# Two expert blocks kept on chip and added by one-hot products, the other rows summed earlier

## What is computed

```python
def hier_moe(x, w_r1, b_r1, w_r2, b_r2, w_gate, w_up, w_down):
    # top-1 group, then top-2 experts of that group: two (expert, gate) pairs for every token
    ...
    def run_block(args):                      # a block: rows of one expert
        tok, e = args
        xb = xpad[tok]
        hidden = jax.nn.silu(xb @ w_gate[e]) * (xb @ w_up[e])
        return hidden @ w_down[e]
    yb = lax.map(run_block, (row_tok.reshape(n_blocks, MOE_BLOCK), blk_expert))
    y = segment_sum(yb * row_gate[:, None], row_tok)[:T]     # each token: sum of its two rows

# for each layer i:
#   x = x + mixer_i(rms_norm(x));  x = x + hier_moe(rms_norm(x))
```

## Time and profile before

| | |
|---|---|
| runs | 1470.32, 1470.36, 1471.22 us (median 1470.36) |
| the profiled execution | 1471.15 us; span of its instructions 1469.2 us |
| busy | PE 88%, DVE 23%, ACT 21%, POOL 16% |
| memory | 464 MB read, 28 MB written, 335 GB/s over the span |
| TensorE's granted clock, mean | 0.946 of full |

### The profile page before, as it was taken

One profiled execution on the slowest core, in us unless ns is written; L12 is line 12 of the kernel. 1 busy time (PEld: TensorE's weight loads), 2 busy tenths in 40 slices (PEclk: granted clock), 3 DMA queues, 4 the chain that ended last, 5 costly groups with the idle time before them and its releaser, 6 DMA issues. The chain is left out here.

```text
span 1469.2 us, 17145 instructions
## 1 busy us (share of the span) xinstructions
PE 1286.6 (88%) x6316; PEld 650.9 (44%) x6316; DVE 344.4 (23%) x719; ACT 308.6 (21%) x638; POOL 233.3 (16%) x391
## 2 busy tenths in 40 slices
PE   9999888888878889999998999999978887888782
PEld 7643333333333333678776544643333343333331
DVE  4621100000000003654317543611000000000003
ACT  4211111111111113343335432211111111111110
POOL 1111111111111102033232220111111111111100
PEclk9999999999999999999999999999998999999997
DMA  9799999999999998412047213999999999999995
GB/s 370 280 361 396 401 397 407 414 412 402 409 408 407 399 415 321 145 58 88 31 136 258 77 31 138 386 375 398 399 406 408 409 411 413 412 404 401 405 401 206
DMA packets 57484, 477.39 MB, mean 325 GB/s; under 512 B 11373, under 2 KB 12653, under 8 KB 31258
## 3 DMA queue, kind: packets, MB, share of 16 engines
q1 hardware_dynamic: 39134, 433.74, 73.5%
q0 software_dynamic: 15504, 33.98, 7.3%
q10 hardware_dynamic: 2796, 8.97, 1.7%
HBM read 464.34 MB, written 28.04 MB: 335 GB/s over the span
## 5 line engine op out<-in xcount | busy, mean ns | idle before, releaser
L1774 PE MATMUL ps<-ring,xT 128*64 128x512 f32 x352 | 182.2, 678 | 48.9 <-issue 40.5
L1444 DVE SCALAR_TENSOR_TENSOR nat<-nat,slot_gate,ps 64x512 f32<-64x512 f32 x64 | 47.3, 739 | 664.9 <-ACT nat L1004 664.7
L1774 PE MATMUL ps<-pair,xT 128*64 128x512 f32 x352 | 169.9, 640 | 37.2 <-DMA pair<-in_moe_w_up 37.2
L1774 PE MATMUL ps<-third_pair,xT 128*64 128x512 f32 x320 | 156.9, 648 | 45.5 <-issue 25.1
L1775 PE MATMUL ps<-ring,xT 128*64 128x512 f32 x352 | 182.6, 679 | 0.0
L707 POOL DMA_INDIRECT yb<-nat,scol x64 | 59.4, 928 | 775.0 <-DVE nat L1440 775.0
L1775 PE MATMUL ps<-pair,xT 128*64 128x512 f32 x352 | 170.4, 641 | 0.0
L1004 ACT ACTIVATE nat<-ps 64x512 f32<-64x512 f32 x64 | 38.0, 594 | 609.5 <-PE ps L1775 609.5
L1775 PE MATMUL ps<-third_pair,xT 128*64 128x512 f32 x320 | 157.3, 649 | 0.0
L1783 PE MATMUL ps<-qk,hidT 128*64 128x512 f32 x336 | 153.1, 598 | 1.2 <-ACT hidT L981 1.2
L1784 PE MATMUL ps<-qk,hidT 128*64 128x512 f32 x336 | 153.2, 598 | 0.0
(11 more groups left out here) (226 smaller groups left out, 1833.0 us busy)
## 6 DMA issues: line engine op xcount, KB each, us to landing
qk<-in_moe_w_down SPq DMA_DIRECT2D x42, 2048.0 KB, 40.1
ring<-in_moe_w_down SPq DMA_DIRECT2D x22, 2048.0 KB, 40.1
pair<-in_moe_w_gate SPq DMA_DIRECT2D x22, 2048.0 KB, 34.6
pair<-in_moe_w_up SPq DMA_DIRECT2D x22, 2048.0 KB, 39.1
ring<-in_moe_w_gate SPq DMA_DIRECT2D x20, 2048.0 KB, 34.4
ring<-in_moe_w_up SPq DMA_DIRECT2D x20, 2048.0 KB, 38.9
third_pair<-in_moe_w_gate SPq DMA_DIRECT2D x20, 2048.0 KB, 34.9
third_pair<-in_moe_w_up SPq DMA_DIRECT2D x20, 2048.0 KB, 39.4
```

The lines of the kernel that those rows point to most:

```text
L1444: return V.scalar_tensor_tensor(out=hidden, in0=silu, scalar=slot_gate[:, bass.ds(j, 1)], in1=ps[0:BLK, GU_BANK, :], op0=ALU.mult, op1=ALU ...
L1774: mm(ps[BLK:P, GU_BANK, :], rows, gate[:, at], start=(k == 0), stop=(k == KT - 1))
```

## The change

1. The last two blocks of each layer, 30 and 31, are no longer scattered. Block 30's rows go to partitions 0 to 63 of `late_y` (a part of `nat`), block 31's to partitions 64 to 127. For each token tile, PE multiplies a one-hot matrix of 128 slots by the tile's tokens (`late_hot`) with `late_y`, two products of 128x512, and DVE adds the result from PSUM to `x` (`late_sum`). DVE builds the one-hot matrix in block 1 (`late_rows`, seven small operations).
2. Since rows of those two experts are no longer written to `yb`, the buffer has to hold zeros there: `yb` is cleared by two DMAs for a layer (`cleared`, 1088 rows, 4.46 MB). Layer 0's stand on SP's queue behind the inputs and before the first weights; layer 1's stand before the fourth piece of `w_qkv`. They read zeros that POOL writes by a memset.
3. POOL raises `rows_scattered` when block 29's rows have landed. `load_rows` loads tiles 0, 1 and 3 then, and tiles 2 and 4 once block 30's result is there. There are five buffers now. In layer 0 the loads stand before the second piece of `w_qkv`, and not before the third; the third waits for `x_done` of three tiles.
4. The sum of a token's two rows is made by DVE for tiles 0, 2 and 4 (`early_sum`) and by POOL for tiles 1 and 3 (`POOL_TILES`); DVE adds it to `x`. In layer 0 these sums stand between the quarters of `split_att`.
5. In layer 0, 12 of 18 `keep_busy` products go, three tiles' one-hot products come in their place, and the other two tiles' stand inside the first product.

```diff
-        yc = [nat[:, 0:2 * D], nat[:, 2 * D:4 * D], qk_flat[:, route_at:route_at + 2 * D], rows_h[:, 3:5, :].rearrange(
-            "p a d -> p (a d)")]
-        assert NT == len(yc) + 1
+        yc = [third_pair[:, 0, 0:2 * D], third_pair[:, 0, 2 * D:4 * D], ring[:, 2, 0:2 * D],
+              qk_flat[:, 2 * KT * T - SLOT:2 * KT * T - 2 * D], qk_flat[:, 2 * KT * T - 2 * D:2 * KT * T]]
+        assert NT == len(yc) and 2 * KT * T - SLOT >= NT * D - D and SLOT == 4 * D
+        LATE = 2
+        late_y = nat[:, 2 * D:3 * D]
+        assert LATE * BLK == P and (NEXP - LATE) % 2 == 0
...
+        zeros = early_rows[:, 3 * D:4 * D]
+        late_hot = ffn_gain[:, 0:NT * P]
+        late_iota = ffn_gain[:, NT * P:(NT + 1) * P]
+        late_at = ffn_gain[:, (NT + 1) * P:(NT + 1) * P + NT]
...
+        POOL_TILES = (1, 3)
+
+        def cleared(l, zero):
+
+            whole = YROWS // P * P
+            return [(yb_dram[l][0:whole, :].rearrange("(p k) d -> p k d", p=P),
+                     zero.unsqueeze(1).broadcast_to((P, YROWS // P, D))),
+                    (yb_dram[l][whole:YROWS, :], zero[0:YROWS - whole, :])]
+
+        def late_bank(l, i):
+
+            return 2 * (i % 4) if l == 1 else 2 * min(i, 2)
+
+        def late_bank_free(l, i):
+
+            return (i - 3 if i > 3 else 0) if l == 1 else (i if i > 2 else 0)
...
+            sp.wait_ge(zeroed, 1)
+            for rows, source in cleared(0, zeros):
+                sp.dma_start(rows, source).then_inc(yb_cleared, 16)
...
                 sp.wait_ge(rows_scattered, l + 1)
-                for i in range(NT):
+                for i in (0, 1, 3, 2, 4):
                     n = ROWS[i]
-                    if i >= len(yc):
-
-                        sp.wait_ge(x_done[l], i - len(yc) + 1)
-                    sp.dma_start(yc[i % len(yc)][0:n, :], yb_dram[l][2 * i * P:2 * (i * P + n), :].rearrange(
+                    if i == 2:
+
+                        sp.wait_ge(y_ps, l * NEXP + NEXP - 1)
+                    sp.dma_start(yc[i][0:n, :], yb_dram[l][2 * i * P:2 * (i * P + n), :].rearrange(
...
 
-                            sp.wait_ge(y_ps, NEXP - 1)
+                            sp.wait_ge(x_done[0], 3)
                         else:
 
                             sp.wait_ge(split_lo, QUARTERS * (j - 2))
-                        if j == 2:
+                        if j == 1:
                             load_rows(0)
+                        if j == 3:
+                            sp.wait_ge(zeroed, 3)
+                            for rows, source in cleared(1, ffn_gain[:, :]):
+                                sp.dma_start(rows, source).then_inc(yb_cleared, 16)
...
+                pool.wait_ge(yb_cleared, 32 * (l + 1))
                 blocks(pool, body)
-                for j in (NEXP - 2, NEXP - 1):
-                    scatter(l, j, j % 2, j // 2, j)
...
-                    pool.wait_ge(scattered[l][u], 16 * (NEXP // 2))
+                    pool.wait_ge(scattered[l][u], 16 * ((NEXP - LATE) // 2))
                 pool.sem_inc(rows_scattered, 1)
+                for i in POOL_TILES:
+                    pool.wait_ge(yc_in[i], 16 * (l + 1))
+                    pool.tensor_tensor(yc[i][:, 0:D], yc[i][:, 0:D], yc[i][:, D:2 * D], ALU.add).then_inc(pool_sum, 1)
...
+            pool.wait_ge(y_ps, NEXP)
             load_router(1)
             pack_router(1)
+
+            pool.wait_ge(x_done[0], NT)
+            pool.memset(ffn_gain[:, :], 0.0).then_inc(zeroed, 1)
...
+                if l == 0 and i == 3:
+                    act.wait_ge(yb_cleared, 32)
...
-                y_out(l, NEXP - 1, 1, NEXP // 2 - 1, NEXP - 1)
+
+                act.wait_ge(y_ps, l * NEXP + NEXP)
+                act.activation(late_y[BLK:P, 512:D], ps[BLK:P, Y_BANK, :], ACT.Copy).then_inc(y_hi[l], 1)
...
+            def late_rows():
+
+                link(V.tensor_tensor_scan(out=late_iota, data0=f32(counting[:, 1, :]), data1=f32(counting[:, 1, :]),
+                                          initial=-1.0, op0=ALU.mult, op1=ALU.add))
+                link(V.tensor_tensor(late_at[:, 1:NT], late_at[:, 0:1].broadcast_to((P, NT - 1)),
+                                     const("steps")[:, 1:2 * NT - 2:2], ALU.subtract))
+                for i in range(NT):
+                    n = ROWS[i]
+                    last = V.tensor_scalar(late_hot[:, i * P:i * P + n], late_iota[:, 0:n], late_at[:, i:i + 1], None,
+                                           ALU.is_equal)
+                last.then_inc(slots_ready, 1)
+
+            def last_y_out(l):
+
+                dve.wait_ge(y_ps, l * NEXP + NEXP)
+                V.tensor_copy(late_y[BLK:P, 0:512], ps[0:BLK, Y_BANK, :]).then_inc(y_lo[l], 1)
...
-            def combine(l, i):
+                        V.tensor_copy(yb[1][:, 0:512], ps[0:BLK, Y_BANK, :]).then_inc(o_y[l], 1)
+
+            def early_sum(l, i):
 
                 n = ROWS[i]
-                rows = yc[i % len(yc)]
-                dve.wait_ge(yc_in[i], 16 * (l + 1))
-                link(V.tensor_tensor(rows[0:n, 0:D], rows[0:n, 0:D], rows[0:n, D:2 * D], ALU.add))
-                V.tensor_tensor(x[0:n, i, :], x[0:n, i, :], rows[0:n, 0:D], ALU.add).then_inc(x_done[l], 1)
-
-                dve.wait_ge(x_done[l], i + 1)
+                if i in POOL_TILES:
+                    dve.wait_ge(pool_sum, l * len(POOL_TILES) + POOL_TILES.index(i) + 1)
+                else:
+                    dve.wait_ge(yc_in[i], 16 * (l + 1))
+                    link(V.tensor_tensor(yc[i][0:n, 0:D], yc[i][0:n, 0:D], yc[i][0:n, D:2 * D], ALU.add))
+                link(V.tensor_tensor(x[0:n, i, :], x[0:n, i, :], yc[i][0:n, 0:D], ALU.add))
+
+            def late_sum(l, i):
+
+                n = ROWS[i]
+                b = late_bank(l, i)
+                dve.wait_ge(late_ps, l * NT + i + 1)
+                V.tensor_tensor(x[0:n, i, :], x[0:n, i, :], ps[0:n, b:b + 2, :].rearrange("p b c -> p (b c)"),
+                                ALU.add).then_inc(x_done[l], 1)
+
+            def attention_row(i):
+
+                normalise(2, i, rows_h[0:ROWS[i], i, :], gain)
 
             route(0)
             experts(0)
-            split_att(0)
-
-
+            early_sum(0, 0)
+            split_att(0, range(2))
+            early_sum(0, 1)
+            split_att(0, range(2, QUARTERS))
             dve.wait_ge(gain_in, 16)
-            for t in range(NT + 2):
-                if t < NT:
-                    combine(0, t)
-                if 1 <= t <= NT:
-                    normalise(2, t - 1, rows_h[0:ROWS[t - 1], t - 1, :], gain)
-                if t >= 2:
-                    transpose_out(2, t - 2)
+            late_sum(0, 0)
+            early_sum(0, 2)
+            attention_row(0)
+            late_sum(0, 1)
+            late_sum(0, 2)
+            transpose_out(2, 0)
+            early_sum(0, 3)
+            attention_row(1)
+            late_sum(0, 3)
+            transpose_out(2, 1)
+            early_sum(0, 4)
+            attention_row(2)
+            late_sum(0, 4)
+            transpose_out(2, 2)
+            for i in (3, 4):
+                attention_row(i)
+                transpose_out(2, i)
...
+            early_sum(1, 0)
+            early_sum(1, 1)
             for i in range(NT):
-                combine(1, i)
+                late_sum(1, i)
+                if i + 2 < NT:
...
+            def late_product(l, i):
+
+                n = ROWS[i]
+                if i == 0:
+                    pe.wait_ge(slots_ready, 4 * l + 4)
+                    pe.wait_ge(y_lo[l], NEXP)
+                    pe.wait_ge(y_hi[l], NEXP)
+                if late_bank_free(l, i):
+                    pe.wait_ge(x_done[l], late_bank_free(l, i))
+                for hf in range(2):
+                    last = mm(ps[0:n, late_bank(l, i) + hf, :], late_hot[:, i * P:i * P + n],
+                              late_y[:, hf * 512:(hf + 1) * 512], start=True, stop=True)
+                last.then_inc(late_ps, 1)
...
-                keep_busy(18, 4, ident, some)
+                for i in range(3):
+                    late_product(0, i)
+                keep_busy(6, QKT_BANK, ident, some)
                 pe.wait_ge(x_done[0], 1)
                 transposes(2, 0)
-                keep_busy(2, 4, ident, some)
+                keep_busy(2, 0, ident, some)
                 early = NT - 2
                 for i in range(early):
                     pe.wait_ge(hT_sb, NT + i + 1)
@@ -1930,6 +2043,8 @@
                         if i == 0:
                             pe.wait_ge(split_lo, q + 1)
                         last = token_quarter(i, i, q)
+                        if q == 0 and i < 2:
+                            late_product(0, 3 + i)
...
+            for i in range(NT):
+                late_product(1, i)
```

More of the change, by code:

```diff
@@ L365, in encoder @@
         rows_scattered = sem("rows_scattered")
+        yb_cleared = sem("yb_cleared")
+        late_ps = sem("late_ps")
+        pool_sum = sem("pool_sum")
```

(11 more changed lines are left out.)

36 lines of the change are left out of this document (19 added, 17 removed).

## The result

The changed kernel took 1478.14 us (median of 22 runs, 1474.03 to 1482.46), the kernel before 1470.83 (22 runs, 1466.99 to 1479.09). The ratio is 1.004, 95% interval 1.0027 to 1.0054: slower by 5.9 us, between 4.0 and 7.9. (The two medians alone lie 7.3 apart; I go by the ratio and its interval.) Measured once more beside two experiments it was 1.0029 (1.0014 to 1.0045), which is 4.3 us. Slower was forecast, by 4.1 us.

The account below looks back on a forecast made before the run. Weight loads bound both expert phases; only the start, layer 0's passage to the attention and the end can move. Terms 0 + 6.2 - 2.1 = +4.1 give 1475.25 us profiled, 1474.5 as median; range 1465 to 1479.

Parts of the forecast that it names:

- Collision of POOL and DVE: Both layers' ends: POOL's sums and DVE's two-input additions block each other; 4.8 us in layer 0, 1.3 and 2.4 at the end.
- First product: Layer 0's end: PE starts the attention's product at 595.1, +2.7 us against before, with the collision counted.
- Without the collision: Layer 0's end if POOL doesn't hold DVE: PE starts the attention's product at 590.3, 2.1 us earlier than before.
- One-hot products inside: Layer 0's attention product: two tiles' 4 products of 0.87 are paid in full on PE, +3.5 us.
- The wait of 1.07 comes from the same chain as before and stays: Layer 0's attention, PE before 611.54 (tile 4's transposes): the wait of 1.07 us is unchanged.
- layer 0's end: From layer 0's experts into the attention: 2.7 for the product's later start plus 3.5 for one-hot products, +6.2 us.
- End: Layer 1's end: rows load earlier, DVE's last addition ends at 1464.75 against 1466.81, -2.1 us with the collision.
- Start: Kernel's start: layer 0's clear, 11.4 us of transfer, is hidden by idle DMA time and idle products; 0, range 0 to 2.
- What lies around the sums: 4.3 us behind DVE's last addition and around the span, left as they are.
- The clear of layer 1: Attention phase, where the memory rate is a third of full or less: the clear costs 0.

Follow-up runs that it names:

- e3: Changed kernel with each of POOL's sums replaced by a POOL memset of 128x2048, which only writes; 1473.82 us in one execution.
- e1: Changed kernel with no sums on POOL, DVE making all five tiles' sums in both layers; 1473.38 us, ratio 1.0004 to the kernel before.
- e2: Changed kernel without the one-hot products of tiles 3 and 4 inside layer 0's attention product; 1474.32 us, ratio 0.9998 to the kernel before.
- e5: Changed kernel without POOL's sums, and DVE scaling tile 4's rows ahead of tile 3's hT_lo; 1474.16 us, ratio 1.0003 to the kernel before.
- e4: Layer 0 of the kernel before; layer 1 as changed, but all sums on DVE, tile 0's ahead of the last copy; 1471.18 us, ratio 0.998.
- e7: Changed kernel with both layers' clears at the start, ahead of the first weights; 1484.63 us, ratio 1.0084 to the kernel before.

## Why the prediction was right, step by step

- **Collision of POOL and DVE**: right in mechanism and nearly in size, 4.3 of holding for 4.8 in layer 0. On the path it was worth 3.2 (e3), since an unheld DVE runs into tile 2's rows. e1 and e3 show it from two sides: take POOL's sums away, or only their reading, and the first product comes 2.7 or 3.2 us earlier.
- **First product**: +1.2 in place of +2.7. DVE was held 0.5 less, tile 0's sum began 2.3 behind the last copy and not 2.6, and an addition from PSUM has a step of 1.13 to 1.14, not 1.25. Against the four traces of the old layer 0 it is +1.1 to +2.3. Without the collision (e3) it is 21.87, which is 0.9 to 2.1 under those four, where -2.1 was forecast.
- **One-hot products inside**: 3.7 for 3.5; e2 shows 3.5 on PE.
- **"The wait of 1.07 comes from the same chain as before and stays"**: this step failed. The new order on DVE puts tile 4's scaled rows behind `hT_lo` of tile 3; the wait is 2.34, and e5 takes the 1.2 back. It made good what the step before had too much, so layer 0's end came to +6.4 where +6.2 was forecast. That the sum was better than its terms is luck.
- **End**: -2.8 for -2.1. The holding was 1.7 and 2.0 there, together the 3.7 forecast (1.3 and 2.4); the branch took 0.2 and not 0.5, and the steps were a little shorter. Tile 1's rows landed 0.3 behind the start of the copy, nearly as computed. Tile 3's and tile 2's landed 4.0 and 7.7 behind it, where 2.7 and 5.4 were computed. It cost nothing here, because the held DVE came to tile 2 only at 9.5; in e4 it is the next bound.
- **Start**: 0 was taken, 0 to 2 as range. At the full clock the ring's loads came at 82.33 to 83.45 in four traces with one clear and at 81.33 in the one without: 1 to 2 us, the upper part of the range. In a fifth (e5) they came at 85.66: PE had waited 1.49 for the gather there, and its next products took 1.08 in place of 0.61. At the lower clock the chain is later and the clear shows no cost (85.5 to 87.0 with it, 85.1 to 87.7 without, three traces each). By layer 0's last copy little or nothing is left of it: 568.3 to 569.6 in those four traces, 568.5 in the one without; at the lower clock 570.9 to 574.1 with it and 572.5 to 574.9 without.
- **What lies around the sums** was left as it is; it grew by 0.5, of which 0.4 lies outside the span (2.25 on average in 22 runs, 1.87 in the kernel before). The rest of the way from +4.1 to +5.9 stays open; the second measurement, 4.3, needs none.
- **The clear of layer 1**: 0, as forecast. From tile 4's transposes to layer 1 it took 355.6 to 360.4 in eleven traces with it, and 359.07 and 358.04 in the two without.

## What to carry to other kernels

Before work is given to an engine that stands idle, look at what both engines read: two additions with both inputs in SBUF, one on DVE and one on POOL, took turns here, and the offload made the stretch longer. Where early data let an engine start sooner, the next bound is the order in which the data land; add up in that order. And a change made to two places is two changes: here one half won 3.4 us and the other lost 7.7, which the time of the whole can't tell.

## What was not expected of the hardware

The start varied by 4 us for identical code. The logits came at 57.27 in the kernel before and at 61.62 in e4, whose start is the same; the granted clock of the first 20 us was 1.00 in the one and 0.89 in the other:

```profile
0.00:20.00 20.00, 14.69 (x60) 10.41 (x60) 5.31 (x8) 6.84 (x12) 0.88 (x7) 0.89 0.90 315
```

Seven of the thirteen traces of this study had a lower one (0.85 to 0.90). The delay is still there at layer 0's last copy: 568.3 to 572.3 in the six traces with a full start, 570.9 to 574.9 in six of the seven with a lower one (the seventh is e7). How much of the 8 us over which runs of one kernel spread comes from it isn't shown, but it is a reason to compare stages rather than ends. What makes one execution start lower than another stays open.
